# Four PSUM banks for the units, evacuations behind the roots, and gate columns summed in 16 halves

## The chip, the cores and the metric

The kernel runs on one core of a Trainium2 chip. A core has five engines that work side by side, each through its own list of instructions in order: TensorE (PE, matrix products), VectorE (DVE), ScalarE (ACT), GpSimd (POOL) and SyncE (SP), which here only issues transfers. They meet through semaphores. TensorE writes its products into eight PSUM banks of 128 partitions by 512 float32 values; bank numbers below are theirs. The metric is the time of one execution on the device in microseconds.

## The reference, cut to what matters

One layer of a mixer over 2048 positions (plus 256 of context) and 1024 channels. The normalised input is projected to 2304 columns, which feed three branches; their gated outputs are projected back.

```python
hx = rmsnorm(x, g_pre) * (1 + sc_x) + sh_x
ux = einsum('bnd,de->bne', hx, w_in)            # 18 tiles of 128 columns
xc = dwconv(vx, conv_w, conv_b)                 # width 4
for rev in (False, True):                       # RG-LRU, both directions
    r = sigmoid(xh @ wa + ba); i = sigmoid(xh @ wx + bx)
    log_a = -8 * r * softplus(-lam); a = exp(log_a)
    b = sqrt(-expm1(2 * log_a)) * (i * xc)
    h = linear_scan(a, b, h0, rev)
z = dwconv(v * sigmoid(gg), dw, dw_b)           # width 31, then LayerNorm, silu, product
out = x + gate * rmsnorm(concat(y * silu(g)) @ w_out, g_post)
```

The vector `gate` is silu(c) times the last 1024 columns of w_mod.

## The kernel before, in words

Every float32 product is made of three: each operand is split into a rounded high part and the rest (`mm3`, L1443 to L1445), so one tile product is three matmuls, with a weight load each.

**Units.** A unit is one tile of 128 projected columns for one chunk of 512 positions: 8 blocks of three, 24 matmuls of 512 columns. There are 72 of them, in the order of `UNITS`, and among them 16 "conv" units (15 matmuls of 256 columns) that make the 31-wide convolution from loaded blocks. Each unit's result goes from its bank to a staging slot in SBUF (`evac` on ScalarE, L912 to L917) and from there to DRAM (`store_u`, issued by SyncE, L453). Two banks (0 and 1) and two slots take turns, so TensorE may be at most one whole unit ahead of the evacuation: unit U waits for the evacuation of U-2 (L1443 is where that wait shows).

**Steps.** The recurrent branch runs between the units in 20 steps, `q` 0 to 19: four channel tiles of five steps each, of which the first (`s` = 0) is the context and the rest work on one chunk forwards and one backwards. `GATES_AFTER` says behind which unit TensorE does the 12 matmuls of step q's gates. Their results lie in four banks, r in banks 2, 3 or 6, 7 by turns, i in 4, 5. Then, in step q:

- ScalarE: four sigmoids (L926, L930), the sigmoid of the convolution's gate for the blocks of that step (L958), for each direction two exponentials and a tanh (`decays`, L942 to L944), **one unit's side work**, the two roots (`roots`, L952), and the side work of the other units up to the one before gates q+1. Side work of unit n (`unit_side`) is its evacuation and, ahead of it, where the tables say so, the rounding of the next projection weights (L867) and of the weights of the conv unit four places on (L965). Both wait for their transfers. A change between sigmoid, exp/tanh and root costs a table load, which the trace shows as ACT_TABLE_LOAD.
- VectorE: convolution pieces (L1236, L1120) for the steps to come, the product of the conv block (L1281), `one_minus_a2` (two instructions of L1120 with output `bank`), `scans` (two times L1257, L1267, L1274), and in steps 3, 5 to 17 `gate_sum`.
- GpSimd: the split of step q+1's inputs (L569 to `sph`, L654 to `spl`), i times x (L664), the low parts of weights (L693, L688), and the sum and store of y.
- SyncE: after each `store_u(n)` it does `after_unit(n)`: the next projection weights (512 KB, L415), the next piece for the gate column sums (`wgp`, 512 KB, L484, which waits until the sum of the piece before is done), and blocks and weights of conv units (L473, L459). The conv weights are issued two places ahead of where ScalarE rounds them, the projection weights one place ahead.

When the channel tile changes (q = 4 to 6, 9 to 11, 14 to 16), VectorE has four convolution pieces to make between the scans of the old tile and the splits that gates q+2 wait for; these spans are called transitions below.

After gates 19 comes the tail, in which TensorE does the other units among the LayerNorm, pooling and pointwise products, and then the output projection (768 matmuls).

Of the kernel before, what the change touches and what calls it, by code (L numbers as in the profile page):

```python
# [43 lines left out]
Z_SLOTS = 3  # L44

# [32 lines left out]
GATE_STEP = [3 + 2 * m for m in range(8)]  # L78
# [14 lines left out]
def mixer_kernel(nc, x, ctx, par, w_mod, b_gate, g_post, w_in, gate_w, pool_w, conv_dw, conf_pw, w_out,  # L93
# [6 lines left out]
    with es:  # L100
# [28 lines left out]
        ustage = fixed.take("ustage", [P, 2, CH])  # L129
# [44 lines left out]
        wgp = a3.take("wgp", [P, KD, P])  # L174
# [9 lines left out]
        lsd = past.take("lsd", [P, CH])  # L184
# [61 lines left out]
        pu = bank[0:2]  # L246
        gr = [bank[2:4], bank[6:8]]
# [22 lines left out]
        s_us = [sem(f"u_stored{b}") for b in range(2)]  # L270
# [126 lines left out]
        def _(sp):  # L397
# [43 lines left out]
            def store_u(U):  # L441
                sp.wait_ge(s_ev, U + 1)
                o, c = UNITS[U - N_CU] if U >= N_CU else (None, None)
                if U < N_CU:
                    dst, src = uc_dram[U], ustage[:, U % 2, 0:CTX]
                elif o == "conv":
                    dst, src = cv_dram[c], ustage[:, U % 2, 0:NPH]
                elif ORDER[o] in CONV_TILES:
                    dst = phases(u_dram[ORDER[o]], NPH)[:, :, c * CH // PHASES:(c + 1) * CH // PHASES]
                    src = phases(ustage[:, U % 2, :], CH // PHASES)  # L450
                else:
                    dst, src = u_dram[ORDER[o], :, c * CH:(c + 1) * CH], ustage[:, U % 2, :]
                sp.dma_start(dst, src).then_inc(s_us[U % 2], 16)  # L453
# [7 lines left out]
            def load_conv_z(j):  # L461
# [13 lines left out]
            def after_unit(n):  # L475
# [23 lines left out]
            def load_item(n):  # L499
# [12 lines left out]
                sp.wait_ge(s_us[U % 2], 16 * (U // 2 + 1))  # L512
# [51 lines left out]
        def _(pool):  # L564
# [52 lines left out]
            def load_v(p):  # L617
# [4 lines left out]
                if c == "ctx":  # L622
                    pool.wait_ge(s_us[t % 2], 16 * (t // 2 + 1))
                    g.dma_start(vbuf[:, p % 2, 2:2 + CTX], uc_dram[t]).then_inc(s_v[p % 2], 16)
                else:
                    a, b = max(c * CH - 2, 0), min((c + 1) * CH + 1, SEQ)
                    U = unit_of(V_LRU + t, NCH - 1)
                    for back in (0, 1):
                        pool.wait_ge(s_us[(U - back) % 2], 16 * ((U - back) // 2 + 1))
# [67 lines left out]
            def load_pool(n):  # L697
# [4 lines left out]
                for back in (0, 1):  # L702
                    pool.wait_ge(s_us[(U - back) % 2], 16 * ((U - back) // 2 + 1))
# [8 lines left out]
            def load_ln(n):  # L712
                if n:
                    pool.wait_ge(s_zc, 2 * n)
                else:
                    for U in range(N_CU + CONV_AT[-1] - 1, N_CU + CONV_AT[-1] + 1):
                        pool.wait_ge(s_us[U % 2], 16 * (U // 2 + 1))
# [135 lines left out]
        def _(act):  # L853
# [50 lines left out]
            def evac(U):  # L904
                act.wait_ge(s_pu, U + 1)
                if U >= 2:
                    act.wait_ge(s_us[U % 2], 16 * (U // 2))
                o, c = UNITS[U - N_CU] if U >= N_CU else (None, None)
                if U < N_CU:
                    ins = a.activation(ustage[:, U % 2, 0:CTX], pu[U % 2][:, 0:CTX], ACT.Copy)  # L910
                elif o == "conv":
                    ins = a.activation(ustage[:, U % 2, 0:NPH], pu[U % 2][:, 0:NPH], ACT.Identity,  # L912
                                       bias=par_col("conf_dw_b", c))
                elif ORDER[o] in CONV_TILES:
                    ins = a.activation(phases(ustage[:, U % 2, :], CH // PHASES), by_phase(pu[U % 2][:]), ACT.Copy)
                else:
                    ins = a.activation(ustage[:, U % 2, :], pu[U % 2][:], ACT.Copy)  # L917
                ins.then_inc(s_ev, 1)

            def sigmoids(q):  # L920
# [3 lines left out]
                for d in range(2):  # L924
                    r = gr[q % 2][d][:, 0:n]
# [7 lines left out]
            def decays(q):  # L933
                t, s = divmod(q, NCH + 1)
                n = CTX if s == 0 else CH
                for d in range(2):
# [4 lines left out]
                    r = gr[q % 2][d][:, 0:n]  # L941
# [4 lines left out]
            def roots(q):  # L946
                s = q % (NCH + 1)
                n = CTX if s == 0 else CH
                for d in range(2):
                    act.wait_ge(s_m2, 2 * q + d + 1)  # L950
                    r = gr[q % 2][d][:, 0:n]
                    a.activation(r, r, ACT.Sqrt).then_inc(s_rt, 1)  # L952
# [57 lines left out]
            for q in range(STEPS):  # L1010
# [31 lines left out]
            def ln_root(m):  # L1042
# [3 lines left out]
                a.activation(lsd[:], lvar[:], ACT.Sqrt, bias=lnepsc).then_inc(s_lsd, 1)  # L1046
# [62 lines left out]
        def _(dve):  # L1109
# [584 lines left out]
```

## Time and profile before

| | |
|---|---|
| median of 3 runs | 865.06 us (864.12 to 872.48) |
| the profiled execution | 870.05 us, span 868.2 us |
| TensorE busy in the span | 772.1 us, 89% |
| VectorE, ScalarE, GpSimd busy | 517.9, 455.3, 393.0 us |
| mean granted TensorE clock | 0.956 of full |
| DMA | 130.09 MB, 150 GB/s |

The profiled execution is 5 us above the median of the runs. Busy time of TensorE counts overlapped matmuls once; an instruction's own duration is longer than the spacing to the next. The time between two starts is the better measure of its rate. Evacuations of full tiles are L917 and L915, those of conv units L912.

### The profile page before, as it was taken

Reading aid. Unit: us, or ns where it says so; the run is one execution under the profiler, and the core shown is the slowest. Engines: PE = TensorE matmul, PEld = TensorE weight load, DVE = VectorE, ACT = ScalarE, POOL = GpSimd, SP = SyncE. Lnnn points to the kernel's source line nnn. Section 1 sums busy time; section 2 is a strip of 40 time slices with the busy share of each in tenths; the row PEclk is TensorE's granted clock in tenths of the full one; section 3 lists DMA queues with packets and bytes.
Section 4 is the critical chain, followed back from the end, with each engine's and each line's share of the span. In section 5 each row is a group of like instructions: output and inputs, shape, how many; then the busy total and the mean of one; then the engine's idle time right before and its main releaser. Section 6 shows DMA issues by size and latency. Waiting matters only on the chain.

```text
span 868.2 us, 9916 instructions
## 1 busy us (share of the span) xinstructions
PE 772.1 (89%) x3468; PEld 614.3 (71%) x3468; DVE 517.9 (60%) x716; ACT 455.3 (52%) x749; POOL 393.0 (45%) x405
## 2 busy tenths in 40 slices
PE   6596898999779889889998899699989699999996
PEld 2275687888668768777776787477668478888885
DVE  4389752646873878595776333665534477666633
ACT  4265642887755875766774675334525253434311
POOL 0268553475555763765546446424300235252521
PEclk9897899999988999999998999899999999999999
DMA  9994013245524254343443123344328765858541
GB/s 367 352 298 136 25 38 122 61 105 134 157 70 119 72 165 152 107 129 102 147 143 103 55 92 112 110 134 134 107 80 322 243 222 183 286 170 264 172 134 74
DMA packets 89073, 130.09 MB, mean 150 GB/s; under 512 B 22752, under 2 KB 54112, under 8 KB 87488
## 3 DMA queue, kind: packets, MB, share of 16 engines
q1 hardware_dynamic: 84656, 115.44, 40.7%
q0 software_dynamic: 4368, 14.03, 5.8%
q8 instruction: 27, 0.44, 0.2%
q14 instruction: 22, 0.18, 0.1%
HBM read 91.17 MB, written 38.27 MB: 149 GB/s over the span
## 4 chain that ended last, share of the span: by engine, by line
PE 44%; ACT 15%; DVE 14%; issue 10%; POOL 7%; DMA 6%; SPq 4%; ACTq 0%; POOLq 0%; DVEq 0%
PE bank L1443 14%; PE bank L1444 14%; PE bank L1445 14%; SPq L403 2%; ACT L942 2%; ACT Qb L943 2%; DVE Qb L1267 2%; ACT bank L944 2%; ACT Ib L930 2%; DMA wraw<-in_w_in 2%; DVE gacc L1120 1%; DVE xg L1153 1%; DVE xc L1120 1%; DVE xTl L1171 1%; DVE Ib L1257 1%
## 5 line engine op out<-in xcount | busy, mean ns | idle before, releaser
L1443 PE MATMUL bank<-xTh,wh 128*128 128x512 f32 (+1 forms) x592 | 239.3, 404 | 40.8 <-ACT ustage L917 11.6
L1445 PE MATMUL bank<-xTh,wl 128*128 128x512 f32 (+1 forms) x592 | 236.1, 399 | 0.0
L1444 PE MATMUL bank<-xTl,wh 128*128 128x512 f32 x576 | 231.9, 403 | 0.0
L1443 PEld LDWEIGHTS bank<-xTh,wh 128*128 128x128 f32 x592 | 116.1, 196 | 68.9 <-issue 42.2
L1445 PEld LDWEIGHTS bank<-xTh,wl 128*128 128x128 f32 x592 | 115.5, 195 | 24.7
L1444 PEld LDWEIGHTS bank<-xTl,wh 128*128 128x128 f32 x576 | 112.9, 196 | 23.8 <-issue 0.2
L1443 PE MATMUL bank<-xTh 128*128 128x512 f32 (+1 forms) x272 | 106.8, 392 | 14.1 <-DVE xTl L1391 7.2
L1445 PE MATMUL bank<-xTh,xTl 128*128 128x512 f32 x256 | 99.9, 390 | 0.0
L1444 PE MATMUL bank<-xTl,xTh 128*128 128x512 f32 x256 | 99.7, 390 | 0.0
L917 ACT ACTIVATE ustage<-bank 128x512 f32<-128x512 f32 x56 | 33.5, 600 | 120.1 <-PE bank L1445 116.0
L569 POOL TENSOR_SCALAR xTh<-yb 128x512 fp32r<-128x512 f32 x32 | 19.8, 619 | 122.1 <-DVE yb L1389 122.1
L1443 PEld LDWEIGHTS bank<-xTh 128*128 128x128 f32 x272 | 52.3, 192 | 27.9 <-DVE xTl L1391 8.4
L569 POOL TENSOR_SCALAR sph<-xc 128x512 fp32r<-128x512 f32 (+1 forms) x36 | 22.7, 644 | 101.8 <-DVE xc L1120 52.8
L1100 ACT ACTIVATE sqj<-bank 128x512 f32<-128x512 f32 x32 | 18.8, 595 | 92.5 <-PE bank L1445 92.5
L1445 PEld LDWEIGHTS bank<-xTh,xTl 128*128 128x128 f32 x256 | 48.0, 188 | 10.2
L1444 PEld LDWEIGHTS bank<-xTl,xTh 128*128 128x128 f32 x256 | 48.1, 188 | 9.8 <-issue 0.3
L693 POOL TENSOR_TENSOR wl<-wraw,wh 128x1024 fp32r<-128x1024 f32 x16 | 39.1, 2446 | 22.4 <-ACT wh L867 22.3
L1120 DVE SCALAR_TENSOR_TENSOR bank<-Qb,bank 128x512 f32<-128x512 f32 (+1 forms) x40 | 24.8, 638 | 40.1 <-ACT bank L944 40.0
L569 POOL TENSOR_SCALAR xTh<-fbuf 128x512 fp32r<-128x512 f32 (+1 forms) x40 | 33.4, 854 | 32.5 <-ACT fbuf L901 32.3
L1120 DVE SCALAR_TENSOR_TENSOR xc<-vbuf,prm,xc 128x512 f32<-128x512 f32 (+1 forms) x60 | 46.3, 772 | 2.1
L664 POOL TENSOR_TENSOR Ib<-Ib,xc 128x512 f32<-128x512 f32 (+1 forms) x40 | 46.7, 1189 | 1.1 <-ACT Ib L930 1.0
L1391 DVE TENSOR_TENSOR xTl<-yb,xTh 128x512 fp32r<-128x512 f32 x32 | 31.8, 994 | 23.6 <-POOL xTh L569 23.6
(189 smaller groups left out, 1520.1 us busy)
## 6 DMA issues: line engine op xcount, KB each, us to landing
scratch_u<-ustage SPq DMA_DIRECT2D x72, 256.0 KB, 2.9
wraw<-in_w_in SPq DMA_DIRECT2D x18, 512.0 KB, 4.2
wm<-in_w_mod SPq DMA_DIRECT2D x8, 1024.0 KB, 11.7
xg<-in_x SPq DMA_DIRECT2D x16, 512.0 KB, 8.8
yb<-scratch_y SPq DMA_DIRECT2D x32, 256.0 KB, 3.1
gb<-scratch_u SPq DMA_DIRECT2D x32, 256.0 KB, 4.4
xres<-in_x SPq DMA_DIRECT2D x16, 512.0 KB, 4.8
out<-tout SPq DMA_DIRECT2D x16, 512.0 KB, 2.9
```

The costliest lines, as they stand in the source:

```text
L403: sp.dma_start(rows(g, i, 0, KD), src[i * P:(i + 1) * P, :].rearrange("p (k j) -> p k j", j=P)).then_inc(s_xin[g], 16)
L569: return g.tensor_scalar(dst, src, 1.0, 1.0, ALU.mult, ALU.mult)
L664: g.tensor_tensor(out=I, in0=I, in1=xc_piece(c), op=ALU.mult).then_inc(s_ix, 1)
L693: g.tensor_tensor(out=l, in0=w_raw(w), in1=h.bitcast(f32), op=ALU.subtract).then_inc(s_wlo, 1)
L917: ins = a.activation(ustage[:, U % 2, :], pu[U % 2][:], ACT.Copy)
L930: a.activation(Ib[:, d, 0:n], gi_[d][:, 0:n], ACT.Sigmoid, bias=par_col("lru_bx", 4 * d + t)).then_inc(s_sig, 1)
L1100: a.activation(sqj[:, h * CH:(h + 1) * CH], ob[m % 3][h][:], ACT.Square, accum_out=ss2[:, h:h + 1]).then_inc(s_osq, 1)
L1120: return v.scalar_tensor_tensor(out=out, in0=in0, scalar=sc, in1=in1, op0=op0, op1=op1)
L1391: v.tensor_tensor(out=xTl[:, k, z_cols(c)], in0=z, in1=xTh[:, k, z_cols(c)].bitcast(f32), op=ALU.subtract).then_inc(s_zl, 1)
L1443: mm(out, wh_, xh_, start=first, stop=False)
L1444: mm(out, wh_, xl_, start=False, stop=False)
L1445: return mm(out, wl_, xh_, start=False, stop=last)
```

## The change

Five edits that hang together:

1. The units behind the first eight, up to that of gates 19, use banks 0, 1, 6, 7 in turn (`WIDE`, `PU_BANK`); unit U then waits for the evacuation of U-4. The other units keep two banks.
2. Banks 6 and 7 are taken from r. r now has banks 2 and 3 alone, and `one_minus_a2` writes its result to SBUF (`Qb`), where the root is taken and where the scans read it. Gates q no longer wait for the scans of step q-2 but for `one_minus_a2` of step q-1.
3. Staging has three slots. Room for the third comes from the LayerNorm root's buffer, which is now its PSUM bank, and from `wgp`, which holds half as much.
4. So the gate column sums come in 16 halves of four instructions, in steps 3 to 18 one each, with a transfer of 256 KB each.
5. In each step ScalarE does all side work of units behind the roots.

```diff
@@ tables
+U_SLOTS = 3
+WIDE = range(N_CU + 2 * NCH, N_CU + GATES_AFTER[-1] + 1)
+PU_BANK = [(0, 1, 6, 7)[U % 4] if U in WIDE else U % 2 for U in range(N_CU + len(UNITS))]
+
+def evacuations_before(U):
+
+    earlier = [V for V in range(U) if PU_BANK[V] == PU_BANK[U]]
+    return earlier[-1] + 1 if earlier else 0
+
-GATE_STEP = [3 + 2 * m for m in range(8)]
+GATE_STEP = [3 + m for m in range(16)]
@@ buffers
-        ustage = fixed.take("ustage", [P, 2, CH])
+        ustage = fixed.take("ustage", [P, U_SLOTS, CH])
-        wgp = a3.take("wgp", [P, KD, P])
+        wgp = a3.take("wgp", [P, KD // 2, P])
-        lsd = past.take("lsd", [P, CH])
-        pu = bank[0:2]
-        gr = [bank[2:4], bank[6:8]]
+        pu = [bank[b] for b in PU_BANK]
+        gr = bank[2:4]
@@ SyncE, after_unit
-                for m in range(KD):
+                for m in range(2 * KD):
                     if n == GATE_PIECE_AT[m]:
                         if m:
                             sp.wait_ge(s_ga, m)
-                        sp.dma_start(wgp[:], w_mod[8 + m // 2, :, :, m % 2 * P:m % 2 * P + P]).then_inc(s_wg, 16)
+                        b, h = divmod(m, 2)
+                        part = w_mod[8 + b // 2, :, h * KD // 2:(h + 1) * KD // 2, b % 2 * P:b % 2 * P + P]
+                        sp.dma_start(wgp[:], part).then_inc(s_wg, 16)
@@ ScalarE
-                if U >= 2:
-                    act.wait_ge(s_us[U % 2], 16 * (U // 2))
+                if U >= U_SLOTS:
+                    act.wait_ge(s_us[U % U_SLOTS], 16 * (U // U_SLOTS))
...
-                    r = gr[q % 2][d][:, 0:n]
-                    a.activation(r, r, ACT.Sqrt).then_inc(s_rt, 1)
+                    root = Qb[:, d, 0:n]
+                    a.activation(root, root, ACT.Sqrt).then_inc(s_rt, 1)
...
-                first = n
                 decays(q)
-                while n < min(first + 1, upto):
-                    unit_side(n)
-                    n += 1
                 roots(q)
                 while n < upto:
                     unit_side(n)
...
-                a.activation(lsd[:], lvar[:], ACT.Sqrt, bias=lnepsc).then_inc(s_lsd, 1)
+                a.activation(lvar[:], lvar[:], ACT.Sqrt, bias=lnepsc).then_inc(s_lsd, 1)
@@ VectorE
-                    r = gr[q % 2][d][:, 0:n]
-                    stt(r, Qb[:, d, 0:n], 1.0, r, ALU.add, ALU.mult).then_inc(s_m2, 1)
+                    stt(Qb[:, d, 0:n], Qb[:, d, 0:n], 1.0, gr[d][:, 0:n], ALU.add, ALU.mult).then_inc(s_m2, 1)
...
-                    link(v.tensor_tensor(out=I, in0=I, in1=gr[q % 2][d][:, 0:n], op=ALU.mult))
+                    link(v.tensor_tensor(out=I, in0=I, in1=Qb[:, d, 0:n], op=ALU.mult))
...
-                acc = gacc[:, m * P:(m + 1) * P]
-                link(v.tensor_scalar(acc, wgp[:, 0, :], cs[:, 0:1], None, ALU.mult))
-                for k in range(1, KD - 1):
-                    link(stt(acc, wgp[:, k, :], cs[:, 2 * k:2 * k + 1], acc, ALU.mult, ALU.add))
-                k = KD - 1
-                stt(acc, wgp[:, k, :], cs[:, 2 * k:2 * k + 1], acc, ALU.mult, ALU.add).then_inc(s_ga, 1)
+                b, h = divmod(m, 2)
+                acc = gacc[:, b * P:(b + 1) * P]
+                for k in range(KD // 2):
+                    scale = cs[:, 2 * (h * KD // 2 + k):2 * (h * KD // 2 + k) + 1]
+                    if h == 0 and k == 0:
+                        ins = v.tensor_scalar(acc, wgp[:, k, :], scale, None, ALU.mult)
+                    else:
+                        ins = stt(acc, wgp[:, k, :], scale, acc, ALU.mult, ALU.add)
+                    if k < KD // 2 - 1:
+                        link(ins)
+                ins.then_inc(s_ga, 1)
+                dve.wait_ge(s_ga, m + 1)
...
-                link(v.reciprocal(lsd[:], lsd[:]))
+                link(v.reciprocal(lvar[:], lvar[:]))
@@ TensorE
-                if U >= 2:
-                    pe.wait_ge(s_ev, U - 1)
+                if evacuations_before(U):
+                    pe.wait_ge(s_ev, evacuations_before(U))
...
-                if q >= 2:
-                    pe.wait_ge(s_st, 2 * (q - 1))
+                    pe.wait_ge(s_m2, 2 * q)
...
-                        pe.wait_ge(s_st, 2 * (STEPS - 1))
+                        pe.wait_ge(s_m2, 2 * STEPS)
...
-                        pe.wait_ge(s_lsd, n)
+                        pe.wait_ge(s_lzn, 2 * n)
...
+                    else:
+                        pe.wait_ge(s_ev, WIDE.stop)
```

Edit 5 on ScalarE, in step 13 (places 47 to 50 of `UNITS`, a conv unit at 48). Before, from the last decay instructions to the next sigmoid:

```order
L944 ACTIVATE bank<-bank,sml 128x512
L965 ACTIVATE cvwh<-cvwraw 128x640 [waits unit_done,convw_in0]
L917 ACTIVATE ustage<-bank 128x512 [waits u_stored1,unit_done]
L952 ACT_TABLE_LOAD
L952 ACTIVATE bank<-bank 128x512 [waits one_minus_a2] x2
L912 ACTIVATE ustage<-bank,prm 128x256 [waits u_stored0,unit_done]
L917 ACTIVATE ustage<-bank 128x512 [waits u_stored1,unit_done]
L867 ACTIVATE wh<-wraw 128x1024 [waits unit_done,w_raw_in1]
L965 ACTIVATE cvwh<-cvwraw 128x640 [waits unit_done,convw_in1]
L917 ACTIVATE ustage<-bank 128x512 [waits u_stored0,unit_done]
L926 ACT_TABLE_LOAD
```

In the changed kernel the same stretch:

```order
L956 ACTIVATE bank<-bank,sml 128x512
L964 ACT_TABLE_LOAD
L964 ACTIVATE Qb<-Qb 128x512 [waits one_minus_a2] x2
L977 ACTIVATE cvwh<-cvwraw 128x640 [waits unit_done,convw_in0]
L929 ACTIVATE ustage<-bank 128x512 [waits u_stored0,unit_done]
L924 ACTIVATE ustage<-bank,prm 128x256 [waits u_stored1,unit_done]
L929 ACTIVATE ustage<-bank 128x512 [waits u_stored2,unit_done]
L879 ACTIVATE wh<-wraw 128x1024 [waits unit_done,w_raw_in1]
L977 ACTIVATE cvwh<-cvwraw 128x640 [waits unit_done,convw_in1]
L929 ACTIVATE ustage<-bank 128x512 [waits u_stored0,unit_done]
L938 ACT_TABLE_LOAD
```

The roots have moved ahead of the first cast and evacuation; nothing else has changed places.

Edit 4 on SyncE, in step 8 (places 30, a conv unit, to 32), with the last stores of step 7 ahead. Before:

```order
L453 DMA scratch_u<-ustage 128x512 [waits unit_evacuated] x2
L453 DMA scratch_cv<-ustage 128x256 [waits unit_evacuated]
L484 DMA wgp<-in_w_mod 128x8x128 [waits gate_summed]
L459 DMA cvwraw<-in_conv_dw 128x640 [waits unit_done]
L473 DMA cvz<-scratch_u 128x256 [waits u_stored0,u_stored1,unit_done]
L473 DMA cvg<-scratch_u 128x256 [waits u_stored0,u_stored1]
L453 DMA scratch_u<-ustage 128x512 [waits unit_evacuated]
L415 DMA wraw<-in_w_in 128x1024 [waits unit_done,w_lo]
L453 DMA scratch_u<-ustage 128x512 [waits unit_evacuated]
L453 DMA scratch_cv<-ustage 128x256 [waits unit_evacuated]
L459 DMA cvwraw<-in_conv_dw 128x640 [waits unit_done]
```

and in the changed kernel, to the start of step 9:

```order
L463 DMA scratch_u<-ustage 128x512 [waits unit_evacuated] x2
L463 DMA scratch_cv<-ustage 128x256 [waits unit_evacuated]
L496 DMA wgp<-in_w_mod 128x4x128 [waits gate_summed]
L469 DMA cvwraw<-in_conv_dw 128x640 [waits unit_done]
L483 DMA cvz<-scratch_u 128x256 [waits u_stored2,u_stored1,u_stored0,unit_done]
L483 DMA cvg<-scratch_u 128x256 [waits u_stored0,u_stored1,u_stored2]
L463 DMA scratch_u<-ustage 128x512 [waits unit_evacuated]
L425 DMA wraw<-in_w_in 128x1024 [waits unit_done,w_lo]
L463 DMA scratch_u<-ustage 128x512 [waits unit_evacuated]
L463 DMA scratch_cv<-ustage 128x256 [waits unit_evacuated]
L496 DMA wgp<-in_w_mod 128x4x128 [waits gate_summed]
L469 DMA cvwraw<-in_conv_dw 128x640 [waits unit_done]
```

A gate piece that waits for `gate_summed` stands in every step from 3 to 17, instead of in every second, ahead of the step's other loads. The sum that it waits for was made in the step before; by `GATE_STEP` and `GATE_PIECE_AT` it is now the one of the same step.

## Rows read from the trace of the kernel before

**Rows 1.** Page: span and TensorE's busy share

```profile
span 868.2 us, 9916 instructions
PE 772.1 (89%) x3468; PEld 614.3 (71%) x3468; DVE 517.9 (60%) x716; ACT 455.3 (52%) x749; POOL 393.0 (45%) x405
```

**Rows 2.** Waits of TensorE, 142 to 523 us: total us, times, longest

```profile
PE bank L1443 <- ACT ustage L917: 11.6, 7, 2.6
PE bank L1443 <- ACT ustage L915: 11.2, 2, 6.8
PE bank L1443 <- ACT ustage L912: 10.8, 5, 3.9
```

**Rows 3.** Timeline of TensorE: start us, us; behind a stall, and 11 us later

```profile
261.58 0.63 PE L1444 MATMUL bank<-xTl,wh 128*128 128x512 f32 x1
262.01 0.63 PE L1445 MATMUL bank<-xTh,wl 128*128 128x512 f32 x1
...
272.81 0.39 PE L1444 MATMUL bank<-xTl,wh 128*128 128x512 f32 x1
273.03 0.39 PE L1445 MATMUL bank<-xTh,wl 128*128 128x512 f32 x1
```

**Rows 4.** Timeline of ScalarE: step 8, from its gates to the next

```profile
294.94 1.24 ACT L926 ACTIVATE bank<-bank,prm 128x512 f32<-128x512 f32 x2 [0.87 <-PE bank L1445]
...
302.42 0.51 ACT L912 ACTIVATE ustage<-bank,prm 128x256 f32<-128x256 f32 x1
...
304.23 1.07 ACT L952 ACTIVATE bank<-bank 128x512 f32<-128x512 f32 x2
...
311.48 1.06 ACT L867 ACTIVATE wh<-wraw 128x1024 fp32r<-128x1024 f32 x1 [5.66 <-DMA wraw<-in_w_in]
312.44 0.72 ACT L965 ACTIVATE cvwh<-cvwraw 128x640 fp32r<-128x640 f32 x1
...
314.96 1.24 ACT L926 ACTIVATE bank<-bank,prm 128x512 f32<-128x512 f32 x2
```

**Rows 5.** Timeline of ScalarE: first sigmoid of steps 6, 7, 11 and 19

```profile
249.34 1.24 ACT L926 ACTIVATE bank<-bank,prm 128x512 f32<-128x512 f32 x2 [0.88 <-PE bank L1445]
...
278.29 1.24 ACT L926 ACTIVATE bank<-bank,prm 128x512 f32<-128x512 f32 x2
...
356.14 1.24 ACT L926 ACTIVATE bank<-bank,prm 128x512 f32<-128x512 f32 x2 [0.88 <-PE bank L1445]
...
518.12 1.24 ACT L926 ACTIVATE bank<-bank,prm 128x512 f32<-128x512 f32 x2 [0.88 <-PE bank L1445]
```

**Rows 6.** Timeline of SyncE's queue in step 16

```profile
462.05 0.55 SPq L484 DMA_DIRECT2D wgp<-in_w_mod  x1
462.64 0.65 SPq L459 DMA_DIRECT2D cvwraw<-in_conv_dw  x1
...
464.57 6.82 SPq L453 DMA_DIRECT2D scratch_u<-ustage  x2
```

**Rows 7.** Timeline of ScalarE: the cast of what that queue loaded

```profile
467.53 0.74 ACT L965 ACTIVATE cvwh<-cvwraw 128x640 fp32r<-128x640 f32 x1 [2.98 <-DMA cvwraw<-in_conv_dw]
```

**Rows 8.** Timeline of VectorE: scans of step 13, a gate sum of step 15

```profile
406.48 0.69 DVE L1257 TENSOR_TENSOR Ib<-Ib,bank 128x512 f32<-128x512 f32 x1 [2.01 <-ACT bank L952]
...
411.17 0.15 DVE L1274 COPY sml<-Qb 128x1 f32<-128x1 f32 x1
...
453.93 0.28 DVE L1295 TENSOR_SCALAR gacc<-wgp,sml 128x128 f32<-128x128 f32 x1
454.25 2.67 DVE L1120 SCALAR_TENSOR_TENSOR gacc<-wgp,sml,gacc 128x128 f32<-128x128 f32 x7
```

**Rows 9.** Timeline of GpSimd: the splits that gates 6 wait for

```profile
243.38 2.53 POOL L654 TENSOR_TENSOR spl<-xc,sph 128x512 fp32r<-128x512 f32 x2
```

**Rows 10.** Groups by line and form, VectorE: count, busy us, mean ns

```profile
L1257 DVE TENSOR_TENSOR Ib<-Ib,bank 128x512 f32<-128x512 f32 x32 | 21.8, 681 | 15.8 <-ACT bank L952 12.1 <-POOL Ib L664 3.3
...
L1281 DVE TENSOR_TENSOR cvz<-cvz,cvg 128x256 f32<-128x256 f32 x16 | 15.4, 975 | 25.8 <-ACT cvg L958 25.6
```

More of the change, by code:

```diff
@@ L269, in mixer_kernel @@
         s_pu, s_ev = sem("unit_done"), sem("unit_evacuated")
-        s_us = [sem(f"u_stored{b}") for b in range(2)]
+        s_us = [sem(f"u_stored{b}") for b in range(U_SLOTS)]
         s_gz, s_gw, s_gwh, s_gwl = sem("gatew_zeroed"), sem("gatew_in"), sem("gatew_hi"), sem("gatew_lo")
@@ L444, in store_u @@
                 if U < N_CU:
-                    dst, src = uc_dram[U], ustage[:, U % 2, 0:CTX]
+                    dst, src = uc_dram[U], ustage[:, U % U_SLOTS, 0:CTX]
                 elif o == "conv":
-                    dst, src = cv_dram[c], ustage[:, U % 2, 0:NPH]
+                    dst, src = cv_dram[c], ustage[:, U % U_SLOTS, 0:NPH]
                 elif ORDER[o] in CONV_TILES:
                     dst = phases(u_dram[ORDER[o]], NPH)[:, :, c * CH // PHASES:(c + 1) * CH // PHASES]
-                    src = phases(ustage[:, U % 2, :], CH // PHASES)
+                    src = phases(ustage[:, U % U_SLOTS, :], CH // PHASES)
                 else:
-                    dst, src = u_dram[ORDER[o], :, c * CH:(c + 1) * CH], ustage[:, U % 2, :]
-                sp.dma_start(dst, src).then_inc(s_us[U % 2], 16)
+                    dst, src = u_dram[ORDER[o], :, c * CH:(c + 1) * CH], ustage[:, U % U_SLOTS, :]
+                sp.dma_start(dst, src).then_inc(s_us[U % U_SLOTS], 16)
             def load_conv_w(j):
@@ L627, in load_v @@
                     U = unit_of(V_LRU + t, NCH - 1)
-                    for back in (0, 1):
-                        pool.wait_ge(s_us[(U - back) % 2], 16 * ((U - back) // 2 + 1))
+                    for back in range(U_SLOTS):
+                        pool.wait_ge(s_us[(U - back) % U_SLOTS], 16 * ((U - back) // U_SLOTS + 1))
                     off = a - (c * CH - 2)
@@ L701, in load_pool @@
                 U = unit_of(V_POOL + i, NCH - 1)
-                for back in (0, 1):
-                    pool.wait_ge(s_us[(U - back) % 2], 16 * ((U - back) // 2 + 1))
+                for back in range(U_SLOTS):
+                    pool.wait_ge(s_us[(U - back) % U_SLOTS], 16 * ((U - back) // U_SLOTS + 1))
                 a, b = max(c * CH - PH, 0), min((c + 1) * CH + PH, SEQ)
@@ L715, in load_ln @@
                 else:
-                    for U in range(N_CU + CONV_AT[-1] - 1, N_CU + CONV_AT[-1] + 1):
-                        pool.wait_ge(s_us[U % 2], 16 * (U // 2 + 1))
+                    for U in range(N_CU + CONV_AT[-1] + 1 - U_SLOTS, N_CU + CONV_AT[-1] + 1):
+                        pool.wait_ge(s_us[U % U_SLOTS], 16 * (U // U_SLOTS + 1))
                 part = slice(n * CH // PHASES, (n + 1) * CH // PHASES)
@@ L924, in sigmoids @@
                 for d in range(2):
[L925 removed]
+                    r = gr[d][:, 0:n]
                     a.activation(r, r, ACT.Sigmoid, bias=par_col("lru_ba", 4 * d + t)).then_inc(s_sig, 1)
@@ L1368, in ln_norm @@
                 dve.wait_ge(s_lsd, n + 1)
-                link(v.reciprocal(lsd[:], lsd[:]))
+                link(v.reciprocal(lvar[:], lvar[:]))
                 for i in range(2):
                     z = lr[:, n % 2, i, :]
-                    v.tensor_tensor(out=z, in0=z, in1=lsd[:], op=ALU.mult).then_inc(s_lzn, 1)
+                    v.tensor_tensor(out=z, in0=z, in1=lvar[:], op=ALU.mult).then_inc(s_lzn, 1)
             def ln_lo(n):
@@ L1507, in gates @@
                     pe.wait_ge(s_sig, 4 * q)
-                if q >= 2:
-                    pe.wait_ge(s_st, 2 * (q - 1))
+                    pe.wait_ge(s_m2, 2 * q)
                 for m in range(4):
                     d = 0 if s == 0 else m // 2
-                    b = gi_[m // 2] if m % 2 else gr[q % 2][m // 2]
+                    b = gi_[m // 2] if m % 2 else gr[m // 2]
                     ins = mm3(b[:, 0:n], gwh[:, m, :], gwl[:, m, :], sph[:, d, 0:n], spl[:, d, 0:n], True, True)
@@ L1583, in gate_row @@
             def gate_row():
-                pe.wait_ge(s_ga, KD)
+                pe.wait_ge(s_ga, 2 * KD)
                 pe.wait_ge(s_ev, N_CU + len(UNITS))
```

23 lines of the change are left out of this document (11 added, 12 removed).

## The prediction

> **What bounds the kernel now.** I read the page first: TensorE is busy for 772.1 of 868.2 us [rows 1], so what can be won at once is what it waits for. Its waits between 142 and 523 us, the part with the 20 steps, come next [rows 2]. They are nearly all for evacuations: 11.6 + 11.2 + 10.8 = 33.6 us in 14 stalls. The timeline then shows what a long stall costs beside itself [rows 3]: just behind one that ended at 261 us, matmuls start 0.43 us apart (261.58 to 262.01), later 0.22 to 0.23 us (272.81 to 273.03). The granted clock had fallen to its lower level, 1.2 instead of 2.4 GHz, while TensorE idled. If half of the 14 stalls are long enough for that, at some ten slow matmuls each, it is 2 us each, 14 in all. The stalls that edit 1 aims at are worth 33.6 + 14 = about 48 us.
>
> Why is the evacuation late? ScalarE's timeline over a whole step [rows 4]: sigmoids at 294.94, first evacuation at 302.42, roots until 305.30, directly behind them the next evacuation, then 5.66 us of waiting for projection weights, two casts, the last evacuation, and the next step's sigmoids at 314.96. ScalarE needs 20.0 us for this step. TensorE's own work in it is two units, one conv unit and the gates: 2 x 24 x 0.227 + 15 x 0.114 (half the columns) + 12 x 0.227 = about 15.4 us. So ScalarE, with its wait for a transfer, is as near to being the bound as TensorE. That is where I look next: what does the change do to that wait?
>
> **Edits 1 and 3, banks and slots.** Nothing is added to any engine. TensorE may be three units ahead of the last evacuation instead of one, 16 us instead of 5, which covers ScalarE's 12 us without evacuation. Alone this takes most of the 48 us. It can't take the 6.8 us stall of [rows 2] before gates 6: those gates need the splits that end at 243.38 + 2.53 = 245.91 [rows 9]. The sigmoids behind them began at 249.34 [rows 5], 3.4 us later, of which 2.9 are the gates' own matmuls. In that transition VectorE's four pieces are the bound. With its slow clock, 8 us stay.
>
> **Edit 2.** Four gate banks become two for r. Gates q+1 now wait for one_minus_a2 of step q. That comes 8.3 us behind the step's first sigmoid: 7.5 to the instruction behind the tanh (302.42 less 294.94 [rows 4]) and 0.8 for the handover and one_minus_a2 itself, an instruction of the size of the multiply in [rows 10]. If ScalarE starts with the gates' end it is 11.3 us from their start, under TensorE's 14 to 23 us per step, and free. If ScalarE is late, TensorE now waits with it at every step, which it did not before. The root in SBUF I cost at nothing: same instructions, same sizes. VectorE's multiply takes 0.68 us with one operand in PSUM [rows 10]; with both in SBUF the nearest row is the conv block's product. That takes 0.975 us on average for half the elements, since some are held up. Ends: 0 and some 0.5 us per multiply; I take 0, because most multiplies fall where GpSimd is idle, and keep the other end as a rival.
>
> **Edit 5.** The first cast and evacuation come 2.35 us later (table load 1.3 between 302.93 and 304.23, roots 1.07 [rows 4]), and the roots 0.5 us earlier. Where the evacuation releases a weight transfer that ScalarE then waits for, the whole step is 2 us longer. This hits steps 1 and 3, which TensorE's work (2 units and the gates, 13.6 us) just covers today. From there through the transition I put +3: sigmoids of step 6 at 252 instead of 249.3 [rows 5].
>
> **Edit 4, the one that decides.** In each step from 3 on SyncE stores the first unit behind the gates and then waits for a gate sum before it issues anything else. Before, that sum was of the step before and long done: at 462.05 the piece went out at once, the conv weights 0.6 us later, and the cast that needs them ran at 467.53 [rows 6, 7], 4.9 us from issue. Now the sum is of the same step. It follows the scans, which follow the roots. ScalarE meanwhile does its evacuations in a burst and comes at once to a cast whose transfer is in the queue behind that wait. The next evacuation, and the next step's sigmoids, stand behind the cast. So ScalarE's period in such a step becomes a chain:
>
> - sigmoids to the end of the roots: 305.30 - 294.94 less the 0.5 us evacuation = 9.8 [rows 4]
> - scans behind the roots: 4.4 (roots' end about 406.9, last copy ends 411.32) [rows 8]
> - half a gate sum: eight instructions take 453.93 to 456.92 = 3.0, so 1.5 [rows 8]
> - gate piece, then the weights' issue: 0.6; issue to cast: 4.9 [rows 6, 7]
> - cast 0.65, last evacuation 0.6, table load 1.3: 2.5 [rows 4]
>
> Sum 23.7 us. Where projection weights are also loaded behind it (steps 8, 13, 15), add 2 us of queue and 1 of cast: 27. It holds where the tables put both the load of conv weights behind the step's gate piece and their cast into the same step: steps 7, 8, 9, 13, 14, 15, 16 (step 6 nearly so, with the projection weights).
>
> **The sum.** I follow the first sigmoid of each step and start each at the later of ScalarE's chain and the gates' end; gates wait for TensorE's units, the splits, or one_minus_a2. From step 6 at 252 TensorE gains first, 4 us by gates 7. But ScalarE is held by step 6's projection weights to 284 (278.3 before [rows 5]), then by conv weights: step 8 at 308 (294.9), step 9 at 335 (315.0, both [rows 4]). In step 9 the conv unit waits for its low part on GpSimd, and the last unit for an evacuation behind the roots, so TensorE stands still too; step 10 starts at 361. The second transition ends with step 11 at 379 (356.1), 23 late. Steps 11 to 13 are free of the wait and run at TensorE's rate: 394, 410, then 438, 13 to 18 late. Steps 14 to 16 are held again: 462, 487, step 17 at 512. The last three run free: step 19 at 540, against 518.12 [rows 5]. So the middle ends 22 us later, though the 48 us of stalls are largely gone; rounding the chain up to 23.7 adds 1. The tail keeps its chains; the LayerNorm root in PSUM I cost at nothing, its users are short of work there (bounds -1 and +3). **Sum +23 us**: 893 on the profiled execution's 870.05, which was 5 us above the median; on the median 865 + 23 = **888 us**.
>
> **Rivals.** *Faster, the banks decide (0.08).* The weights land before ScalarE comes to the cast, as they would if its evacuations still had to wait for TensorE: the point is whether the burst ends earlier than 12 us behind the roots. For it: in the long steps (5 units) they do wait. Then 48 - 8 - 3 for the rest of the transitions = 37 us are won: 828. *Faster, in part (0.08).* The SyncE wait binds but later steps recover more than I give them; half the held steps cost nothing: about 850. *No change (0.10).* What banks win the wait takes, 857 to 873. *Slower by contention (0.12).* The multiply with both operands in SBUF is held up while GpSimd works: VectorE's conv product shows it, 0.975 us for 256 columns where 0.68 is the time of 512 [rows 10]. At 0.5 us for each of two multiplies, in the ten steps whose chain runs through the scans, +10: 898, and up to 905. The Trainium skill, "SBUF — State Buffer", section "Who interferes with whom", states that a VectorE instruction with two SBUF inputs contends with a GpSimd instruction that reads SBUF, and one with a single SBUF input does not. By that rule this rival would be the forecast; the trace agrees so far as the PSUM form never shows it (mean 0.681 us in 32). *Forecast (0.62).*
>
> **Numbers.** Forecast's own range: the issue-to-cast time may be 1 us less or the gate sum 1 us more in each of these eight steps, 877 to 899. To leave out no more than 2 in 10 I reach down into the partial case and up into contention: 856 to 904. One per cent, 8.7 us, is about what a measurement can tell from no change. Faster by more 0.16, within 0.10, slower 0.74.
>
> **What would show it.** In the changed profile: TensorE's waits for evacuations down from 33.6 us to under 15; a new wait of the gates' first matmul for one_minus_a2; ScalarE's waits for the conv weights 40 us or more in all; SyncE's gate pieces issued 6 to 7 us behind the roots; steps 7 and 8 of 23 us or longer from sigmoid to sigmoid. I am wrong if the casts follow the roots within 5 us, or if step 9 starts before 315.

## The result, and the profile after

| | before | after |
|---|---|---|
| median | 867.33 us (4 runs, 864.12 to 872.48) | 910.84 us (4 runs, 908.73 to 912.54) |
| profiled execution, span | 870.05, 868.2 us | 911.04, 909.4 us |
| TensorE busy, granted clock | 772.1 us, 0.956 | 778.7 us, 0.929 |

The ratio is 1.0495, interval 1.0433 to 1.0557: 43.5 us slower, where 23 were forecast. The page answers to [rows 1]:

```profile
span 909.4 us, 9955 instructions
...
PE 778.7 (86%) x3468; PEld 622.8 (68%) x3468; DVE 518.7 (57%) x716; ACT 455.7 (50%) x749; POOL 398.2 (44%) x405
```

No engine has more work worth speaking of. The waits between 142 and 570 us (total, times, longest), of TensorE, ScalarE and SyncE's queue:

```profile
PE bank L1456 <- DVE Qb L1128: 30.1, 5, 10.1
PE bank L1456 <- POOL cvwl L700: 23.1, 3, 11.2
PE bank L1456 <- POOL spl L666: 21.3, 3, 9.5
...
ACT wh L879 <- DMA wraw<-in_w_in: 76.2, 8, 18.0
ACT cvwh L977 <- DMA cvwraw<-in_conv_dw: 41.2, 4, 12.2
...
SPq L496 <- DVE gacc L1128: 104.1, 15, 13.7
```

TensorE's waits for evacuations, 33.6 us in [rows 2], are gone. In their place it waits 74.5 us for `one_minus_a2`, the low parts of the conv weights and the splits. SyncE's queue stands 104.1 us before gate pieces, and ScalarE waits 117.4 us for weights.

Step 6 has the longest such wait. The casts in these rows are the roundings of weights to their high part (`wh` of projection weights, `cvwh` of conv weights). ScalarE's timeline from its first sigmoid to step 7's (start, duration, in brackets the idle time before):

```profile
254.25 1.24 ACT L938 ACTIVATE bank<-bank,prm 128x512 f32<-128x512 f32 x2 [3.71 <-PE bank L1458]
...
264.30 1.15 ACT L964 ACTIVATE Qb<-Qb 128x512 f32<-128x512 f32 x2
265.36 0.72 ACT L977 ACTIVATE cvwh<-cvwraw 128x640 fp32r<-128x640 f32 x1
...
266.92 0.60 ACT L927 ACTIVATE ustage<-bank 128x512 f32<-128x512 f32 x1
285.51 1.06 ACT L879 ACTIVATE wh<-wraw 128x1024 fp32r<-128x1024 f32 x1 [18.00 <-DMA wraw<-in_w_in]
...
289.00 1.24 ACT L938 ACTIVATE bank<-bank,prm 128x512 f32<-128x512 f32 x2
```

VectorE and SyncE's queue in the same step:

```profile
268.46 1.78 DVE L1295 TENSOR_TENSOR cvzl<-cvz,cvzh 128x256 fp32r<-128x256 f32 x1 [4.75 <-POOL cvzh L581]
270.16 0.68 DVE L1264 TENSOR_TENSOR Ib<-Ib,Qb 128x512 f32<-128x512 f32 x1
...
274.61 2.02 DVE L1128 SCALAR_TENSOR_TENSOR gacc<-wgp,sml,gacc 128x128 f32<-128x128 f32 x4
```

```profile
261.07 6.04 SPq L463 DMA_DIRECT2D scratch_u<-ustage  x2
276.66 0.39 SPq L496 DMA_DIRECT2D wgp<-in_w_mod  x1
277.09 0.50 SPq L463 DMA_DIRECT2D scratch_cv<-ustage  x1
277.64 0.43 SPq L469 DMA_DIRECT2D cvwraw<-in_conv_dw  x1
...
279.76 0.69 SPq L425 DMA_DIRECT2D wraw<-in_w_in  x1
```

Read them backwards: the cast at 285.51 wants `wraw`, issued at 279.76. That stood behind the gate piece of 276.66, which waited for the half sum that ended at 276.63, and that followed the scans. The evacuations had long been over, at 267.5. This is the chain that was forecast.

The first sigmoid of each step, before, as forecast and after:

| step | 6 | 7 | 8 | 9 | 10 | 11 | 12 | 13 | 14 | 15 | 16 | 17 | 19 |
|---|---|---|---|---|---|---|---|---|---|---|---|---|---|
| before | 249.3 | 278.3 | 294.9 | 315.0 | 339.9 | 356.1 | 375.9 | 395.8 | 419.1 | 435.3 | 453.4 | 481.8 | 518.1 |
| forecast | 252 | 284 | 308 | 335 | 361 | 379 | 394 | 410 | 438 | 462 | 487 | 512 | 540 |
| after | 254.3 | 289.0 | 313.7 | 340.2 | 363.9 | 384.7 | 400.2 | 424.5 | 455.4 | 481.0 | 505.8 | 530.2 | 558.9 |
| after less forecast | 2.3 | 5.0 | 5.7 | 5.2 | 2.9 | 5.7 | 6.2 | 14.5 | 17.4 | 19.0 | 18.8 | 18.2 | 18.9 |

Of the 41 us by which step 19 is late, 22 were forecast. Most of the missing 19 arise in three places: 5 up to step 7, 8.3 in step 12, and 4.5 in steps 13 and 14. The tail takes 350.5 us from there, 350.1 before.

### The profile page after: what moved, and what is told of

Its sections match the earlier page's. It is cut to its first block, busy times and chain, and to the rows that moved or that the text cites. A ratio compares the mean times of both kernels' runs of the same rounds, so it can differ in the third digit from the quotient of the medians.

```text
span 909.4 us, 9955 instructions
## 1 busy us (share of the span) xinstructions
PE 778.7 (86%) x3468; PEld 622.8 (68%) x3468; DVE 518.7 (57%) x716; ACT 455.7 (50%) x749; POOL 398.2 (44%) x405
## 4 chain that ended last, share of the span: by engine, by line
PE 44%; DVE 13%; ACT 12%; issue 10%; DMA 8%; POOL 7%; SPq 5%; POOLq 0%; ACTq 0%; DVEq 0%
PE bank L1456 14%; PE bank L1457 13%; PE bank L1458 13%; DMA wraw<-in_w_in 3%; SPq L413 2%; DVE Ib L1264 2%; DVE Qb L1274 2%; ACT Ab L954 1%; POOL Ib L676 1%; ACT L954 1%; DVE gacc L1128 1%; ACT Qb L955 1%; DVE yrow L1274 1%; ACT Ib L942 1%; POOL spl L666 1%
## 5 line engine op out<-in xcount | busy, mean ns | idle before, releaser
L1456 PE MATMUL bank<-xTh,wh 128*128 128x512 f32 (+1 forms) x592 | 234.2, 396 | 6.2 <-POOL wl L705 3.6
L1458 PE MATMUL bank<-xTh,wl 128*128 128x512 f32 (+1 forms) x592 | 232.3, 392 | 0.0
L1457 PE MATMUL bank<-xTl,wh 128*128 128x512 f32 x576 | 228.1, 396 | 0.0
L1458 PEld LDWEIGHTS bank<-xTh,wl 128*128 128x128 f32 x592 | 113.5, 192 | 23.8
L1457 PEld LDWEIGHTS bank<-xTl,wh 128*128 128x128 f32 x576 | 110.5, 192 | 23.1 <-issue 0.2
L1456 PE MATMUL bank<-sph,gwh 128*128 128x512 f32 (+1 forms) x80 | 35.3, 442 | 51.4 <-DVE Qb L1128 30.1
L879 ACT ACTIVATE wh<-wraw 128x1024 fp32r<-128x1024 f32 x18 | 19.0, 1054 | 90.9 <-DMA wraw<-in_w_in 90.9
L1108 ACT ACTIVATE sqj<-bank 128x512 f32<-128x512 f32 x32 | 18.9, 596 | 85.9 <-PE bank L1458 85.9
L1456 PEld LDWEIGHTS bank<-sph,gwh 128*128 128x128 f32 x80 | 18.1, 226 | 58.0 <-issue 32.0
L581 POOL TENSOR_SCALAR sph<-xc 128x512 fp32r<-128x512 f32 (+1 forms) x36 | 25.3, 717 | 73.8 <-DVE xc L1128 54.7
L1128 DVE SCALAR_TENSOR_TENSOR Qb<-Qb,bank 128x512 f32<-128x512 f32 (+1 forms) x40 | 25.1, 632 | 43.5 <-ACT bank L956 43.3
```

Source lines behind the costliest of these rows:

```text
L581: return g.tensor_scalar(dst, src, 1.0, 1.0, ALU.mult, ALU.mult)
L879: a.activation(W_JOBS[w][1][0], w_raw(w), ACT.Copy).then_inc(s_whi, 1)
L1108: a.activation(sqj[:, h * CH:(h + 1) * CH], ob[m % 3][h][:], ACT.Square, accum_out=ss2[:, h:h + 1]).then_inc(s_osq, 1)
L1128: return v.scalar_tensor_tensor(out=out, in0=in0, scalar=sc, in1=in1, op0=op0, op1=op1)
L1456: mm(out, wh_, xh_, start=first, stop=False)
L1457: mm(out, wh_, xl_, start=False, stop=False)
```

## The experiments

The theory ("W" in the expectations): the new place of the gate piece, in the queue ahead of the weights and behind a sum of the same step, costs the time. The rivals: the other edits do, by contention of the multiply in SBUF or by the gates' new wait ("C"), or the wait hides a cost that stays without it.

**The gate piece at the step's end.** In the changed kernel:

```diff
-GATE_PIECE_AT = [GATES_AFTER[q - 1] + 1 for q in GATE_STEP]
+GATE_PIECE_AT = [GATES_AFTER[q] for q in GATE_STEP]
```

and the issue of blocks and conv weights stands ahead of the gate piece's in `after_unit`.

> The changed kernel with one thing different: SyncE issues each gate piece at the end of a step (behind the store of the unit ahead of the next gates, last of that unit's issues) instead of behind the first store of the step, so that nothing is queued behind its wait for the step's own sum. Theory W (that wait holds the weights back, and with them ScalarE): SyncE's waits for the sums fall from 104 us to under 15, ScalarE's waits for weight transfers from 117 us to about 40, and the time from 911 to 840 to 865. Rival C (the cost is contention of the multiply in SBUF and the gates' wait for one_minus_a2, whatever SyncE does): stays above 890.

Measured: 866.99 us, 0.9984 (0.9953 to 1.0015). So the place of these small transfers costs 44 us, all that the change loses. The other edits together neither gain nor lose. Three numbers missed what was expected: the time is 2 us above the range, SyncE still stands 47.2 us before gate pieces (under 15 expected), and ScalarE still waits 59.9 us for weights (about 40 expected). What SyncE still waits lies at the ends of steps, with no load of the same step behind it.

**The halves alone**, in the kernel before (16 half pieces at the changed kernel's places, and the half sums):

> The kernel before with edit 4 alone: gate columns in 16 halves, a piece behind the first store of each step from 3 on, waiting for the same step's sum. Two banks, two slots, roots and evacuations as before. Theory W: slower than before by 15 to 40 us (880 to 905), SyncE waits 80 us or more for the sums and ScalarE's waits for transfers double. Rival C: as before, 862 to 872, since neither the root's place nor the gates' wait has changed.

Measured: 926.49 us, 1.0668 (1.0621 to 1.0714), SyncE 133.3 us before gate pieces, ScalarE 102.6 us for the two kinds of weights (32.2 before). The wait needs no other edit. It costs 59 us here, more than in the changed kernel and more than was expected.

**Evacuation ahead of the roots again**, in the kernel of the first experiment:

```diff
+                first = n
                 decays(q)
+                while n < min(first + 1, upto):
+                    unit_side(n)
+                    n += 1
                 roots(q)
```

> The late piece kernel with edit 5 undone: one unit's side work stands between the exponentials and the roots again. Theory W with my cost of edit 5 (weights are asked for 2.3 us later where ScalarE waits for them): 3 to 8 us faster than the late piece kernel. Rival (with four banks the evacuation's place does not matter and the roots are what VectorE waits for): same within 2 us or slower, as the scans start 0.6 to 2 us later.

Measured: 858.10 us, 0.9880 (0.9843 to 0.9916). Edit 5 costs 9 us with four banks.

**Two banks**, in the kernel of the first experiment:

```diff
-PU_BANK = [(0, 1, 6, 7)[U % 4] if U in WIDE else U % 2 for U in range(N_CU + len(UNITS))]
+PU_BANK = [U % 2 if U in WIDE else U % 2 for U in range(N_CU + len(UNITS))]
```

> The late piece kernel with edit 1 undone: all units in banks 0 and 1. It shows what the banks are worth once SyncE does not hold anything. If they are worth the 33.6 us of stalls and the slow clock behind them, this one is 30 to 50 us slower than the late piece kernel and slower than before, as its evacuations are behind the roots. If TensorE is held by the gates' inputs anyway, under 15 us slower.

Measured: 910.01 us, 1.0484 (1.0443 to 1.0525). Four banks are worth 43 us there; the experiment with the roots first alone, below, shows what against.

**The root in SBUF alone**, in the kernel before (`one_minus_a2`, root and multiply use `Qb`):

> The kernel before with the root in SBUF and nothing else: one_minus_a2 writes Qb, the root is taken there and the scans' multiply reads it there; banks, waits, sums and order as before. Theory C (the multiply with two SBUF operands is held up by GpSimd): multiply of 512 columns from 0.68 to 0.85 us or more on average, and, since VectorE's pieces bound the transitions, 3 to 8 us slower. Rival: the stretched multiplies lie where VectorE has slack, same within 2 us.

Measured: 868.77 us, 1.0013 (0.9988 to 1.0039). Groups by form of VectorE, of this kernel and then of the changed one (count, busy us, mean ns), for [rows 10]:

```profile
L1257 DVE TENSOR_TENSOR Ib<-Ib,Qb 128x512 f32<-128x512 f32 x32 | 26.7, 834 | 15.6 <-ACT Qb L952 15.2
```

```profile
L1264 DVE TENSOR_TENSOR Ib<-Ib,Qb 128x512 f32<-128x512 f32 x32 | 27.2, 851 | 12.3 <-ACT Qb L964 9.7 <-POOL Ib L676 2.2
```

The multiply goes from 681 to 834 ns and the kernel takes the same time.

**Roots first alone**, edit 5 in the kernel before (the three lines of `while` go):

> The kernel before with edit 5 alone: all evacuations behind the roots, two banks, two slots, whole gate sums. With two banks each evacuation that comes 2.4 us later is 2.4 us more of TensorE's waiting in every step with a conv unit (14 of them), and the clock falls in more of them: 885 to 905. If the place did not matter with the casts' transfers waited for anyway, under 875.

Measured: 909.86 us, 1.0491 (1.0462 to 1.0520), 5 us above the expected range. TensorE's waits in it, 142 to 570 us:

```profile
PE bank L1440 <- ACT ustage L912: 24.2, 6, 6.3
PE bank L1440 <- ACT ustage L917: 24.0, 6, 5.0
PE bank L1440 <- ACT ustage L915: 17.3, 4, 11.0
```

The same 33.6 us have become 65.5. With two banks each evacuation that moves behind the roots stops TensorE, and ScalarE then waits at the step's end for units that start late. The 43 us of the two-bank experiment are the cure of this, so most of the banks' worth there only pays for edit 5.

**Whole sums**, the changed kernel with edits 3 and 4 undone (two slots, `wgp` whole, 8 sums at their old places), then **whole sums with the evacuation ahead**, edit 5 undone too, so that edits 1 and 2 alone are left:

> The changed kernel with edits 3 and 4 undone: two staging slots, a whole gate piece of 512 KB and eight sums in every second step as before; four banks, root in SBUF, evacuations behind the roots stay. SyncE then never waits for a sum of the same step. Theory W: 855 to 868, at or under the late piece kernel (867.0), which still waited 47 us for sums; ScalarE's waits for weights under 60 us. Rival (the third slot is what carries the burst of evacuations): slower than the late piece kernel by 5 us or more, with ScalarE waiting for stores.

> The kernel of e9 with edit 5 undone too: of the change only the four banks and the root in SBUF remain. From the two late piece kernels (867.0 and 858.1) undoing edit 5 is worth 9 us; with no SyncE wait left I expect 846 to 858, the fastest so far. If SyncE's waits at the end of steps cost nothing, 856 to 860.

Measured: 868.61 us, 1.0008 (0.9992 to 1.0024), and 857.85 us, 0.9891 (0.9865 to 0.9918). The first is at the upper end of what was expected: with two slots ScalarE waits 20.0 us for stores, but the 1.6 us to the kernel with late pieces are less than the runs can tell, so the third slot shows no worth. The second is as fast as the kernel with late pieces and the evacuation ahead (858.10), in which SyncE stands 63.6 us before gate pieces at the ends of steps: that wait costs nothing there. The second has no wait for an evacuation left either, and yet gains only 9.5 us. Its waits of TensorE, 142 to 570 us:

```profile
PE bank L1452 <- POOL spl L664: 12.9, 3, 7.6
PE bank L1452 <- POOL cvwl L698: 11.3, 2, 6.3
...
PE bank L1452 <- DVE Qb L1130: 4.7, 2, 2.4
```

In the kernel before, gates hardly waited for splits (group by form of TensorE, idle time last):

```profile
L1443 PE MATMUL bank<-sph,gwh 128*128 128x512 f32 x64 | 25.1, 392 | 0.7 <-POOL spl L654 0.7
```

Splits, low parts of conv weights and `one_minus_a2` now hold TensorE for 28.9 us, nearly the 33.6 it was freed of: it comes to the next input earlier and stands there.

**The half sum first**, in the changed kernel:

```diff
                 one_minus_a2(q)
+                if q in GATE_STEP:
+                    gate_sum(GATE_STEP.index(q))
                 for j in convs_in_step(q, 4):
                     conv_z_lo(j)
                 scans(q)
-                if q in GATE_STEP:
-                    gate_sum(GATE_STEP.index(q))
```

> The changed kernel, but in VectorE's program each step's half gate sum stands directly behind one_minus_a2, ahead of the scans, instead of behind them; SyncE's queue and all the rest stay. Theory (the wait costs by its length, which is roots, scans and half sum; nothing else about the gate piece's place matters): the sum now ends some 1.5 us behind one_minus_a2, about when the roots do, so the wait on SyncE is 6 to 7 us shorter in each step, SyncE's waits for gacc fall from 133 us in all to under 50, ScalarE's waits for the two kinds of weights from 117 to under 75, and nearly all of the 44 us come back: 867 to 878. Rival A (half of the wait is in what lies before the scans: ScalarE's decays of the same step): waits stay above 80 us, 885 to 900. Rival B (the half sum, now between one_minus_a2 and the scans, delays the scans and everything behind them, the transitions' pieces above all): 5 us or more are lost to that in the transitions, 875 to 885 with SyncE's waits under 50.

Measured: 874.06 us, 1.0052 (1.0026 to 1.0079). SyncE's row becomes

```profile
SPq L496 <- DVE gacc L1128: 9.6, 8, 2.6
```

Nothing has moved in SyncE's queue; 37 of the 44 us come back (38 by the ratios), because the sum is made in time that VectorE otherwise spends waiting, in the changed kernel 9.7 us for the roots and 22.7 for the high part of conv blocks. (The 133 us of the expectation are those of the halves alone; the changed kernel has 104.1.) The cost is the wait's length: that is shown, not only argued.

**Evacuation ahead with the early piece**, the changed kernel with edit 5 alone undone:

> The changed kernel with edit 5 undone: in each step one unit's side work stands ahead of the roots again; the gate pieces stay where the change put them. Theory (edit 5 costs its 9 to 11 us by itself, beside the wait): 899 to 903, SyncE's waits for gacc as long as in the changed kernel or longer. Rival (edit 5 is what makes the wait expensive, since all the step's evacuations then end in front of a cast whose weights are not there): half of the 44 us go with it, 875 to 888.

Measured: 928.1 us, 1.0646 (1.0592 to 1.0700). Both were wrong: edit 5, which costs 9 to 11 us without the wait, saves 13 to 17 with it (by the ratios, by the medians). ScalarE in step 12 of this kernel, where its first sigmoids are at 408.12:

```profile
426.78 1.06 ACT L879 ACTIVATE wh<-wraw 128x1024 fp32r<-128x1024 f32 x1 [6.18 <-DMA wraw<-in_w_in]
...
430.26 1.15 ACT L964 ACTIVATE Qb<-Qb 128x512 f32<-128x512 f32 x2
```

The cast goes with the evacuation. Ahead of the roots, its wait for the transfer delays the roots' end to 23.3 us behind the sigmoids (16.2 in the changed kernel), with it the scans and the next sum, and so the transfers of the step after. In steps 4 to 13 ScalarE waits 23.5 us in this way ahead of the roots, in the changed kernel not once. SyncE stands 161.1 us before gate pieces here. The loop closes on itself. With the halves alone, where one unit's side work is ahead of the roots too, such waits come to 11.5 us; that is a part of why they cost 59 us, and the rest is not taken apart.

The runs lead from one kernel to the other in four steps: edits 1 and 2, 867.3 to 857.9; edit 5, to 868.6; slots and halves with late pieces, to 867.0, which is no difference that the runs can tell; the pieces early, to 910.8.

## Why the prediction was right in kind and wrong in size

- **The deciding edit: right.** The chain through the gate sum was named as what decides, and taking its wait away, in either of two ways, takes the loss away.
- **Its length in the middle steps: right.** The sum of terms was 23.7 us, 27 with projection weights. Measured: 24.7, 26.5 and 23.7 for steps 7 to 9, 25.6, 24.7 and 24.5 for 14 to 16.
- **"Steps 11 to 13 are free of the wait and run at TensorE's rate": the step that failed.** Step 12 was given 16 us and took 24.4. (Step 11 was given 15 and took 15.5.) VectorE from the roots of step 11 (end 396.53) on, then GpSimd's splits beside it:

```profile
399.63 1.79 DVE L1295 TENSOR_TENSOR cvzl<-cvz,cvzh 128x256 fp32r<-128x256 f32 x1 [4.84 <-POOL cvzh L581]
401.34 1.09 DVE L1264 TENSOR_TENSOR Ib<-Ib,Qb 128x512 f32<-128x512 f32 x1
...
405.66 2.19 DVE L1274 TENSOR_TENSOR_SCAN yrow<-Ab,sml,Ib 128x512 f32<-128x512 f32 x1
...
408.07 2.42 DVE L1306 TENSOR_SCALAR gacc<-wgp,sml 128x128 f32<-128x128 f32 x1
410.52 1.12 DVE L1128 SCALAR_TENSOR_TENSOR gacc<-wgp,sml,gacc 128x128 f32<-128x128 f32 x3
```

```profile
402.88 3.88 POOL L666 TENSOR_TENSOR spl<-xc,sph 128x512 fp32r<-128x512 f32 x2
```

  The low part of the conv block waits for its high part on GpSimd and holds up the scans, and GpSimd's instructions stretch what follows. The half sum's end and the gate piece come 15.1 us behind the roots (411.68), not the 5.9 of the sum's terms "4.4" and "1.5": 4.8 pass before the first multiply, the scans take 6.7, and the half sum 3.6, of which its first instruction has 2.42 (0.29 us at 257.12) beside GpSimd's product of i and x (407.85 to 410.39). ScalarE in step 12:

```profile
404.21 0.69 ACT L942 ACTIVATE Ib<-bank,prm 128x512 f32<-128x512 f32 x1 [2.81 <-DVE sml L1281]
408.07 0.69 ACT L942 ACTIVATE Ib<-bank,prm 128x512 f32<-128x512 f32 x1 [3.17 <-DVE sml L1281]
...
415.25 1.15 ACT L964 ACTIVATE Qb<-Qb 128x512 f32<-128x512 f32 x2
420.18 1.06 ACT L879 ACTIVATE wh<-wraw 128x1024 fp32r<-128x1024 f32 x1 [3.78 <-DMA wraw<-in_w_in]
```

  Two things make up the 8.4 us. The second pair of sigmoids writes the buffer that the late scans of step 11 still read: 6.0 us of waiting, which has nothing to do with the gate piece. With the half sum first the step has it too:

```profile
382.13 0.69 ACT L942 ACTIVATE Ib<-bank,prm 128x512 f32<-128x512 f32 x1 [2.83 <-DVE sml L1281]
385.99 0.69 ACT L942 ACTIVATE Ib<-bank,prm 128x512 f32<-128x512 f32 x1 [3.17 <-DVE sml L1281]
```

  The roots end at the same 16.2 us behind the sigmoids there, and the step takes 20.5 us, 4.5 more than it was given. Edits 1 and 2 alone have the wait as well (5.8 us, step 12 in 20.3). The other 3.9 are the wait of step 11 reaching over into step 12, the 3.78 in the row of the cast. The kernel before took 20.0 us for step 12 too, but by another bound. There ScalarE waited for TensorE, behind a stall that the banks remove:

```profile
393.04 0.60 ACT L917 ACTIVATE ustage<-bank 128x512 f32<-128x512 f32 x1 [4.73 <-PE bank L1445]
```

  So the 16 us fit TensorE's own work, as the prediction counts it for a step of two units and a conv unit (15.4 us). What was left out is the wait that appears when the gates no longer hold the step back: the scans of step 11.
- **Steps 13 and 14** took 30.9 and 25.6 us instead of 28 and 24. The sum of step 13 ended 8.8 us behind the roots, that of step 14 6.7.
- **The first transition: 5 us short.** The sum of step 6 ended 11.2 us behind the roots, 4.7 of them before the first multiply for the same low part, and ScalarE was held to 289.0, not 284. Before that, gates 6 waited 9.46 us for the splits and ran at the slow clock. TensorE's timeline:

```profile
248.79 0.80 PE L1456 MATMUL bank<-sph,gwh 128*128 128x512 f32 x1 [9.46 <-POOL spl L666]
...
250.24 0.63 PE L1456 MATMUL bank<-sph,gwh 128*128 128x512 f32 x1
250.66 0.63 PE L1457 MATMUL bank<-spl,gwh 128*128 128x512 f32 x1
...
254.28 0.40 PE L1457 MATMUL bank<-xTl,wh 128*128 128x512 f32 x1
254.51 0.39 PE L1458 MATMUL bank<-xTh,wl 128*128 128x512 f32 x1
```

  Starts lie 0.42 us apart at first (250.24 to 250.66), which is the granted level of 1.2 GHz, and 0.23 later, at 2.4 (granted clock 0.50 from 248.7 to 254.0, 1.00 from there to 260). The twelve took 5.3 us where I had 2.9, about the 2.3 us by which step 6 was late.
- **"Banks alone take most of the 48 us": wrong.** Edits 1 and 2 brought 9.5, since TensorE ran into the 28.9 us of other waits. The forecast hardly used that number, as ScalarE's chain set most steps; the two rivals that ended faster did, and both are refuted. The root in SBUF, which went with the banks, costs nothing that shows.
- **Edit 5, +3: wrong in size.** It costs 9 to 11 us without the wait and saves 13 to 17 with it, an interplay that no part of the sum held.
- **Contention, the rival at 898 to 905: its price exists, its effect mostly not.** The multiply took 0.17 us more on average, not 0.5, and alone it cost nothing that shows (1.0013, interval 0.9988 to 1.0039), though its 40 multiplies took 7.8 us more in all. In the changed kernel they took 8.6 us more; what that does there was not tested apart. The rival's time is nearer to the measured one than the forecast's, by luck. In "SBUF — State Buffer", section "Who interferes with whom", the Trainium skill states that a VectorE instruction with two SBUF inputs contends with a GpSimd instruction that reads SBUF; the trace agrees (681 to 851 ns on average, 1.09 us for the one at 401.34, which began beside a high part of the splits), but what it does to this kernel is in the runs alone. In the steps with late scans the stretched scans, which had two SBUF inputs before the change too, are a part of the 15.1 us.
- **Two slips of the working.** Its own times put steps 12, 13 and 14 at 18, 14 and 19 us late, not "13 to 18", and one us either way in eight steps gives 880 to 896, not "877 to 899". Neither moves the sum.

What was to be seen: waits for evacuations under 15 us (none), a new wait of the gates for `one_minus_a2` (30.1 us), waits for conv weights of 40 us or more (41.2), steps 7 and 8 of 23 us or more (24.7, 26.5), step 9 not before 315 (340.2). Off was that gate pieces follow the roots by 6 to 7 us: 5.5 to 15.1.

## What to carry to other kernels

A wait on an in-order queue of transfers is paid by whatever is queued behind it: before a wait is moved or made more frequent, write down when its condition comes true in that same step, in every kind of step, and what loads stand behind it. There are two ways out. The transfer can be issued where no load of the same step is queued behind it (all of the 44 us come back here), or its condition can be made true earlier (37 of them, by one call moved in VectorE's program). And where a forecast gives a stretch less than it took before, because what bounded it there has gone, look for the next wait of every engine in it, here ScalarE's for the scans of the step before; of a stall removed, count only what lies before the next input is ready.

## What the runs showed of the hardware

- A multiply with both operands in SBUF can be held for as long as a GpSimd instruction runs. Two of 128x256 in the changed kernel, and the GpSimd instruction beside the first:

```profile
253.02 1.77 DVE L1264 TENSOR_TENSOR Ib<-Ib,Qb 128x256 f32<-128x256 f32 x1
...
490.84 0.41 DVE L1264 TENSOR_TENSOR Ib<-Ib,Qb 128x256 f32<-128x256 f32 x1
```

```profile
252.78 1.74 POOL L700 TENSOR_TENSOR cvwl<-cvwraw,cvwh 128x640 fp32r<-128x640 f32 x1
```

  The same instruction takes 0.41 us alone and 1.77 beside it, until GpSimd is done at 254.52 and a little longer. It looks like all or nothing rather than a share: nine of the 40 multiplies were held, and all nine ended 0.28 to 0.29 us (256 columns) or 0.53 to 0.55 us (512) behind the end of the GpSimd instruction that ran when they began. So a mean over a form says little of the worst case, 2.52 us for 512 columns at 542.02.
- The contention goes both ways: two splits took 3.88 us beside VectorE's scans and 2.53 us in [rows 9]; the scan of 405.66 took 2.19 us beside them, and one takes 1.28 in quiet stretches.
- Behind a stall of 9.46 us TensorE paid another 2.5 us: twelve matmuls took 5.3 us at the lower clock level, and the same twelve 2.8 in the kernel before (246.36 to 249.14).
